# A mixture-of-experts encoder block on one core: residual matmuls moved among the routing's waits, the expert mask written in bf16 by a maximum, picks signalled per token tile, the first gathered columns scaled in two halves

## The reference, cut to what matters

```python
logits = rmsnorm(h) @ w_router + b_router           # 32 experts
top_val, top_idx = lax.top_k(logits, 4)
gates = softmax(top_val)
# for every (token, chosen expert): rows in blocks, each block owned by one expert
gu = xb @ w_gate_up[e] + b_gate_up[e]                # 1024 -> 2048
gate, up = split(gu); gate = min(gate, 7); up = clip(up, -7, 7)
out = ((up + 1) * gate * sigmoid(1.702 * gate)) @ w_down[e] + b_down[e]
y[token] += gates[token, e] * out
h = h + y
```

## Time and profile before

| | before |
|---|---|
| median of 3 runs | 1205.65 us (1204.3 to 1206.27) |
| profiled execution: its own time, and its span | 1204.05 us, 1202.3 us |
| busy: TensorE, VectorE, ScalarE, GpSimd | 97%, 25%, 18%, 1% of the span |
| chain that ended last | TensorE 82%, DMA 14%, ScalarE 2%, VectorE 1% |
| mean granted TensorE clock | 0.995 |
| moved by DMA | 440.27 MB, mean 366 GB/s |

### The profile page before, as it was taken

The page is one execution under the profiler, slowest core; times in us unless marked ns, Lnnn a source line. Parts: engine busy times, 40 slices in busy tenths (PEclk is TensorE's granted clock), DMA queues, the critical chain, the costliest instruction groups (busy, mean ns, idle before and its releaser), DMA issues.

```text
span 1202.3 us, 13962 instructions
## 1 busy us (share of the span) xinstructions
PE 1167.2 (97%) x5359; PEld 477.6 (40%) x5359; DVE 302.0 (25%) x681; ACT 214.9 (18%) x404; POOL 6.6 (1%) x13
## 2 busy tenths in 40 slices
PE   9999999999999999999999999899999999999996
PEld 4476556854333333333333333333333333333332
DVE  3457553246221111111211111111111121111112
ACT  2120551221111111111111111011111111111112
POOL 0000010000000000000000000000000000000000
PEclk9999999999999999999999999999999999999999
DMA  9800279337999999999999999999999999999993
GB/s 362 359 1 1 99 274 339 162 141 304 426 429 427 427 431 431 428 433 430 433 429 429 431 428 433 432 431 428 418 436 432 428 428 433 424 427 427 428 426 160
DMA packets 29858, 440.27 MB, mean 366 GB/s; under 512 B 4592, under 2 KB 4848, under 8 KB 11152
## 3 DMA queue, kind: packets, MB, share of 16 engines
q1 hardware_dynamic: 28944, 439.32, 86.6%
q10 hardware_dynamic: 864, 0.19, 0.1%
HBM read 438.45 MB, written 1.05 MB: 366 GB/s over the span
## 4 chain that ended last, share of the span: by engine, by line
PE 82%; DMA 14%; ACT 2%; DVE 1%; issue 0%; POOLq 0%; ACTq 0%; DVEq 0%
PE quad L1516 31%; PE quad L1538 16%; DMA ring<-in_w_gate_up 14%; PE y_banks L1492 5%; PE quad L1476 4%; PE y_banks L1314 2%; PE quad L1128 2%; PE y_banks L1128 2%; PE quad L1484 1%; ACT work L613 1%; PE y_banks L1150 1%; PE y_banks L1220 1%; PE y_banks L1291 1%; PE quad L1299 1%; PE quad L1425 1%; PE y_banks L1425 1%
## 5 line engine op out<-in xcount | busy, mean ns | idle before, releaser
L1516 PE MATMUL quad<-ring,work 128*64 128x512 f32 x2112 | 465.2, 597 | 12.9 <-DMA ring<-in_w_gate_up 12.7
L1516 PEld LDWEIGHTS quad<-ring,work 128*64 128x64 f32 x2112 | 149.9, 138 | 305.5 <-issue 288.8
L1538 PE MATMUL quad<-ring,work 128*64 128x512 f32 x1056 | 233.9, 595 | 4.4
L1538 PEld LDWEIGHTS quad<-ring,work 128*64 128x64 f32 x1056 | 72.9, 137 | 152.2 <-issue 131.9
L1069 DVE TENSOR_SCALAR work<-quad 128x512 f32<-128x512 f32 x33 | 22.8, 692 | 313.8 <-PE quad L1516 313.8
L609 ACT ACTIVATE work<-work 128x512 f32<-128x512 f32 x33 | 20.8, 630 | 444.6 <-DVE work L1069 444.6
L986 DVE CAST work<-cst 96x64 bf16 (+1 forms) x34 | 6.5, 191 | 272.6 <-PE quad L1516 272.6
L1492 PE MATMUL y_banks<-work 64*128 64x512 f32 x272 | 67.6, 615 | 0.7 <-ACT work L619 0.7
L1476 PE MATMUL quad<-h,work 128*64 128x512 f32 x272 | 64.2, 593 | 0.0
L617 ACT ACTIVATE work<-quad 128x512 f32<-128x512 f32 x33 | 19.7, 597 | 237.2 <-PE quad L1538 237.2
L609 ACT ACT_TABLE_LOAD x33 | 42.3, 1283 | 1.1 <-issue 0.5
(11 more groups left out here) (270 smaller groups left out, 825.0 us busy)
## 6 DMA issues: line engine op xcount, KB each, us to landing
ring<-in_w_gate_up SPq DMA_DIRECT2D x37, 4096.0 KB, 33.3
ring<-in_w_gate_up SPq DMA_DIRECT2D x54, 2048.0 KB, 22.9
ring<-in_w_down SPq DMA_DIRECT2D x18, 4096.0 KB, 32.5
ring<-in_w_down SPq DMA_DIRECT2D x28, 2048.0 KB, 22.0
ring<-in_w_mkv SPq DMA_DIRECT2D x8, 1024.0 KB, 23.5
ring<-in_w_in SPq DMA_DIRECT2D x7, 976.0 KB, 17.6
ring<-in_w_o SPq DMA_DIRECT2D x1, 4096.0 KB, 13.0
ring<-in_w_mq SPq DMA_DIRECT2D x1, 4096.0 KB, 22.7
```

The lines of the kernel that those rows point to most:

```text
L1516: ins = mm(bank[n // 2][lo:lo + BLK, :], xgT[:, k % 4 * P + k // 4 * BLK:k % 4 * P + k // 4 * BLK + BLK], up_rows(j, k)[:, n * 512:(n + 1) ...
L1538: ins = mm(bank[3][n * BLK:(n + 1) * BLK, :], lhs, down_rows(j, f)[:, n * 512:(n + 1) * 512], start=(f == 0), stop=(f == KC - 1))
```

## The change

Four edits, all of them at the routing and the start of the first item, two of them with a wait that stands in every item.

- The residual matmuls are issued one half at a time. Tile 0, half 0 goes between the last transposes and the last router matmuls; tile 1, half 0 and tile 0, half 1 go ahead of the rank matmuls; tile 1, half 1 goes behind them. Each has a wait on `h2_ready`.
- The mask is reduced with a maximum straight into bf16. The float32 mask and the cast are gone; the offsets and the gates read the bf16 mask.
- The counts are copied behind the picks. Each tile's pick has a signal of its own, and `gather` waits for each tile's pick before its matmuls.
- The first gathered columns are scaled in two halves, each with a signal. `item` waits for the first half at its start and for the second at k step 2; the counts of this semaphore in the other waits are one higher.

```diff
@@ top_experts @@
-                link(dve.tensor_reduce(mask[:, t, :], oh[t].rearrange("p j e -> p e j"), X, ALU.add))
-                dve.tensor_copy(mask_bf[:, t, :], mask[:, t, :]).then_inc(S["mask_ready"], 1)
-                link(dve.tensor_scalar(unset[:, t, :], mask[:, t, :], BIG, -BIG, ALU.mult, ALU.add))
+                dve.tensor_reduce(mask_bf[:, t, :], oh[t].rearrange("p j e -> p e j"), X, ALU.max).then_inc(S["mask_ready"], 1)
+                dve.wait_ge(S["mask_ready"], t + 1)
+                link(dve.tensor_scalar(unset[:, t, :], mask_bf[:, t, :], BIG, -BIG, ALU.mult, ALU.add))
@@ choose @@
                 for t in range(TT):
-                    ins = dve.tensor_scalar(pick[:, t, :], ...)
-                ins.then_inc(S["pick_ready"], 1)
+                    dve.tensor_scalar(pick[:, t, :], ...).then_inc(S["pick_ready"], 1)
@@ gathered_out @@
-            def gathered_out(w):
+            def gathered_out(w, parts=1):
...
+                m = 4 // parts
+                for i in range(0, 4, m):
+                    dve.tensor_tensor(xgT.rearrange("p (c n s) -> p c n s", c=4, n=2)[:, i:i + m, :, :],
+                                      bank[3][:, :].rearrange("p (c n s) -> p c n s", c=4, n=2)[:, i:i + m, :, :],
+                                      over(halves[:, i:i + m, :].unsqueeze(3), [P, m, 2, BLK]), ALU.mult).then_inc(S["xg_ready"], 1)
@@ VectorE, after the second tile's top_experts @@
             dve.wait_ge(S["rank_mm"], 1)
-            dve.tensor_copy(cnt, bank[3][:, 64:96])
             link(dve.tensor_tensor(place_e, spl(bank[3][:, 0:2 * NE], 2), unset, ALU.add))
             choose(0, 0)
+            link(dve.tensor_copy(cnt, bank[3][:, 64:96]))
             choose_bias(0)
...
-            gathered_out(0)
+            gathered_out(0, 2)
@@ TensorE @@
+            def residual_in(t, n):
+                pe.wait_ge(S["h2_ready"], 2 * t + n + 1)
+                mm(bank[4 + 2 * t + n][:, :], ident, h[:, t, n * 512:(n + 1) * 512], start=True, stop=False,
+                   skip_group_check=True)
...
             router(1, 0)
             columns(1, 1)
+            residual_in(0, 0)
             router(1, 1).then_inc(S["rt_mm"], 1)
-            residual_in(1)
+            residual_in(1, 0)
+            residual_in(0, 1)
...
-            def gather():
+            def gather(w):
                 for t in range(TT):
+                    pe.wait_ge(S["pick_ready"], w * TT + (t + 1))
...
             def item(w, j):
                 pe.wait_ge(S["xg_ready"], w + 1)
                 for k in range(KC):
+                    if k == 2:
+                        pe.wait_ge(S["xg_ready"], w + 2)
...
                 pe.wait_ge(S["gsel_ready"], w + 1)
-                pe.wait_ge(S["pick_ready"], w + 2)
-                gather()
+                gather(w + 1)
...
                 pe.wait_ge(S["hid_ready"], w + 1)
-                pe.wait_ge(S["xg_ready"], w + 2)
+                pe.wait_ge(S["xg_ready"], w + 3)
...
-            residual_in(0)
-            pe.wait_ge(S["pick_ready"], 1)
-            gather()
+            residual_in(1, 1)
+            gather(0)
```

More of the change, by code:

```diff
@@ L270, in encoder_kernel @@
               for i in range(TT)]
-        mask = rt2(384, NE)
         mask_bf = rt[:, 448:448 + NE].bitcast(bf16).rearrange("p (t n) -> p t n", t=TT)
@@ L978, in choose @@
+                dve.wait_ge(S["mask_ready"], t + 1)
+                link(dve.tensor_scalar(unset[:, t, :], mask_bf[:, t, :], BIG, -BIG, ALU.mult, ALU.add))
             def choose(e, off):
                 for t in range(TT):
-                    ins = dve.tensor_scalar(pick[:, t, :], cst[:, bass.ds(off + C_IOTA, BLK)], place_e[:, t, bass.ds(e, 1)],
-                                            stats_of["h2"][3][:, t:t + 1], ALU.is_equal, ALU.mult)
-                ins.then_inc(S["pick_ready"], 1)
+                    dve.tensor_scalar(pick[:, t, :], cst[:, bass.ds(off + C_IOTA, BLK)], place_e[:, t, bass.ds(e, 1)],
+                                      stats_of["h2"][3][:, t:t + 1], ALU.is_equal, ALU.mult).then_inc(S["pick_ready"], 1)
@@ L985, in choose_bias @@
             def choose_bias(e):
                 dve.tensor_copy(bsel[0:96, :], over(cst[0:96, bass.ds(e + C_MOD, 1)], [96, BLK])).then_inc(S["bsel_ready"], 1)
-            def gathered_out(w):
+            def gathered_out(w, parts=1):
                 dve.wait_ge(S["xgT_mm"], w + 1)
                 halves = gain[:, G_MOE:G_MOE + KC].rearrange("p (n c) -> p c n", n=2)
-                dve.tensor_tensor(xgT.rearrange("p (c n s) -> p c n s", c=4, n=2),
-                                  bank[3][:, :].rearrange("p (c n s) -> p c n s", c=4, n=2),
-                                  over(halves.unsqueeze(3), [P, 4, 2, BLK]), ALU.mult).then_inc(S["xg_ready"], 1)
+                m = 4 // parts
[3 more added lines that the diff above has]
+                                      over(halves[:, i:i + m, :].unsqueeze(3), [P, m, 2, BLK]), ALU.mult).then_inc(S["xg_ready"], 1)
@@ L1022, in _ @@
             for t in range(TT):
-                dve.scalar_tensor_tensor(gates_e[:, t, :], ex[:, t, :], ersum[:, t:t + 1], mask[:, t, :], ALU.mult,
+                dve.scalar_tensor_tensor(gates_e[:, t, :], ex[:, t, :], ersum[:, t:t + 1], mask_bf[:, t, :], ALU.mult,
                                          ALU.mult).then_inc(S["gates_ready"], 1)
-            gathered_out(0)
+            gathered_out(0, 2)
             link(dve.tensor_scalar(cum, extra, 1.0, None, ALU.add))
```

## The result

| | before | after |
|---|---|---|
| median of the runs, timed side by side | 1205.56 us (1204.30 to 1206.53, 20 runs) | 1207.96 us (1204.57 to 1209.91, 20 runs) |
| ratio, 95% interval | | 1.0019 (1.0013 to 1.0025) |
| profiled execution: its own time, and its span | 1204.05 us, 1202.3 us | 1205.62 us, 1203.8 us |
| mean granted TensorE clock | 0.995 | 0.997 |
| chain that ended last | TensorE 82%, DMA 14% | TensorE 85%, DMA 10% |

The account below looks back on a forecast made before the run. Up to 820 us it took the weight stream (DMA), started by the first item's up matmuls, as the bound. Gather 1.11, halves 0, item 0 0.1, later items 0: 1.2 off the 1205.65 median, 1204.4 us; range 1202.9 to 1206.4.

Parts of the forecast that it names:

- Residual matmuls: Routing: one call fits ahead of the last router matmuls at no cost, so the gather loses 0.86 us of queue.
- Mask: Routing: without the cast the rank matmuls start 0.20 us sooner, bounds about 0 and 0.20.
- Counts and picks: Routing: later count copy and per-tile picks have the first pick ready at 283.36, before TensorE is free at 283.53 to 283.60.
- The forecast of 1.11: First item's gather: starts at 283.55 instead of 284.66, 1.11 us gained, with TensorE and not the pick setting it.
- Halves: First scaling: operand ready 0.28 us earlier, but taken as nothing because TensorE enters its loop behind the gates' copy.
- at most 0.06: First up matmul: by the skill's branch times, loop entry at 288.78 against operand at 288.72 lets halves buy at most 0.06.
- Item 0: Item 0's gather need not wait for the second pick, so its down chunks release 0.1 us sooner, between 0 and 0.2.
- The stream: Weight transfers to 820 us: an earlier first up matmul starts the stream, the landing and the end earlier by the same amount.
- Later items: Items after 820 us: two more met waits each, 0 to 0.1 per wait, 0 to 2.7 in sum, taken as 0.
- rival 4: Items after 820 us: 27 added waits each expose a weight load of 0.14, 3.8 in all, net +2.6, 1208.2; chance 0.06.
- an item of 26.8 or more: Test after 820 us: an item this long, instead of the forecast 26.7, would make rival 4 right.
- The clock: Last wait for weights: granted clock falls there and slows the kernel; chance 0.09 together with rival 4.

Follow-up runs that it names:

- e6: Kernel before with only the residual matmuls moved as in the change; 1204.43 us in one run.
- e7: Kernel before with only the mask changed (maximum written in bf16, no cast); router to gather 4.76 us against 4.97, total time not used.
- e4: e1 with the first columns scaled whole again by one operation that signals 2; 1203.42 us in one run.
- e5: e1 with TensorE's wait for ScalarE's gates copy moved from before the item loop into the first expert's gathers; 1205.33 us, ratio 1.0004.
- e1: Kernel after with two waits swapped, scaled columns (w + 3) now ahead of hidden values; 1204.38 us against 1205.25 before, ratio 0.9991.
- e8: All four edits, with separate semaphores for the first tile's pick and first scaled half, so item waits keep their old counts; 1203.05 us, ratio 0.9978.
- e3: Kernel after with one more met wait, with its own register sum, behind the wait for hidden values; 1209.55 us in 4 runs, ratio 1.0040.
- e10: Kernel after with the output-bias matmuls moved from expert 28 to expert 12; 1202.71 us, ratio 0.9973.
- e11: Kernel before with the output-bias matmuls moved from expert 28 to expert 12; 1202.81 us, ratio 0.9979.
- e2: Kernel before with the first scaling signalling 2 and the item's last wait asking w + 3, adding one register sum; 1210.01 us, ratio 1.0034.

## Why the prediction was wrong, by its own steps

- **Residual matmuls: right.** A call ahead of the last router matmuls cost nothing (1.44 to 1.44), and one left behind the ranks. e6 gives 0.75 for the move; 0.86 was the call's length. There the gather starts 1.14 behind the remaining call (281.89 to 283.03 in e6), where it starts 1.04 behind it in the kernel after (281.82 to 282.86): in e6 the picks, done at 282.98, come last, and that is where the last 0.11 lay.
- **Mask: right.** 0.20 forecast, 0.21 in e7.
- **Counts and picks: right in their role.** The forecast of 1.11 has no term for them (0.86 and 0.20, and 0.05 in reading the row at 284.66); they had to bring the picks ahead of TensorE's queue. They did, and without them 0.11 of the gain would be missing, if the parts add up. The whole is 1.07 for a forecast of 1.11, with TensorE, not the pick, setting the gather.
- **Halves: right, with the reason.** Nothing forecast; 8.17 with and without them (e4), and e5 shows the loop's entry as what held them back. The estimate that a split costs VectorE 0.12 more came out at 0.07 (0.76 against 0.69). The other estimate, "at most 0.06", was misread: with the loop entered at 288.78, behind the operand's 288.72, the halves would have bought nothing.
- **Item 0: right and taken back.** From the first up matmul to its gather 13.96 before, 13.83 after: 0.13 sooner. But its down matmuls, the ones that refill the queues, come 19.59 behind the first up matmul instead of 19.53, since the sum stands in front of them. In e1 and e8, where it does not, they come at 19.43 and 19.40, the 0.1 of the forecast.
- **The stream: roughly.** The first up matmul was 1.80 sooner in the profiled execution (0.73 of it scatter), the landing 1.10. From the one to the other it is 531.5 us before, 532.2 after, and 531.5 to 531.9 in the experiments, but for e5 (532.6, whose item 0 waits for picks). At most 0.06 of the 0.7 is item 0's, and e3, whose down matmuls come later still (19.68), has 531.6: the rest was not settled.
- **Later items: this step failed.** I costed "two more met waits per item", between 0 and 0.1 each, and took 0. That was right for those two (e8). The third edited line, the count raised from `w + 2` to `w + 3`, I did not cost at all. It added no wait, but a sum behind an unmet one, 0.19 an item and 2.7 in all, more than twice what the routing gives. My rival 4 had the place and a price of the same size (3.8), by a mechanism that isn't there: e8 has both added waits and an item of 26.68. That its 1208.2 lies 0.2 from the measured 1207.96 is luck: the measured loss is 2.7 of sums and a rest that looks like falls. Its test, "an item of 26.8 or more", came true all the same, so that test could not tell the two apart.
- **The clock: underpriced, as far as is known.** I gave a fall at the last wait for weights part of 0.09. In the kernel after falls are the likely account of what is left of the median, some 0.8: 2.4 is -1.1 of routing and landing, 2.7 of sums, and this. That share is a remainder, not a measurement; e10 is what supports it. Likewise e8's median lies 1.4 further down than its profiled execution says, and the fall at the landing, in four of six profiled executions of the older VectorE code and in none of e8's kind, is the likely reason. It wasn't shown for the timed runs.

## What to carry to other kernels

When a semaphore's count changes, look at every wait on it, also at those that gain no wait: a new `counter + constant` can be an instruction of its own, and it belongs ahead of the wait that is met last, or the signal gets a semaphore of its own so that the old value serves. Weigh an edit of a startup, which pays once, against what it puts into the loop behind the last cover, which here paid 14 times. And work that can run in any item, like the output bias, belongs where the transfers are the bound: that one move was worth 2.7 us (e11), about what the four edits together gave at their best (2.4 in e8).

## What the runs showed of the hardware that was not expected

- One register sum between a wait just met and the matmul behind it took 0.19 us, with the slot's wait instruction that it holds back; a further wait with its own sum took 0.10 more. The same kinds of sum in the middle of matmuls that TensorE has queued up (k step 2, the gather) took nothing: e8 has two of them, and an item of 26.68.
- Entering a loop behind a wait cost 0.35 on TensorE: three small instructions about 0.1 apart, none of them a branch. Moving the wait away gave 0.37 (e5).
- A fall of the granted clock to 1.2 GHz cost 1.7 us each time. In the 14 profiled executions, up to the last item, 26 falls came in a wait for weights of 2.0 to 3.5 us or within 1.4 us behind it, and five (two in e2, one each in e5, e10 and e11) at the end of the output-bias matmuls or right behind them, with no gap of over 0.4 us on TensorE in the 12 us before. Whether a fall cost anything was decided by whether a wait for weights came later.
